# Sums of the second down product's weights made in DRAM by accumulating DMAs from GpSimd's queue

## What is computed

```python
# first block
ffn = silu(h2 @ w_ffn_gate) * (h2 @ w_ffn_up) @ w_ffn_down      # (512, 2816) @ (2816, 1024)
x = x + gate2 * ffn
# second block, whose x is the final norm of the first
u = causal_dwconv(rms_norm(h, ffn_norm) @ w_up, conv_w, conv_b)
gate, up = split(u, 2)
h = h + (silu(gate) * up) @ w_down                              # (512, 2816) @ (2816, 1024)
```

## Time and profile before

| | |
|---|---|
| time, median of 3 runs | 1522.67 us (1521.63 to 1524.0) |
| span of the profiled execution | 1520.9 us |
| PE busy | 1499.2 us, 99% |
| DVE busy | 1026.8 us, 68% |
| ACT busy | 661.2 us, 43% |
| POOL busy | 46.2 us, 3% |
| mean granted clock | 0.998 |
| moved by DMA | 229.29 MB, all of the program's own on one queue |

### The profile page before, as it was taken

The page is one execution under the profiler, slowest core; times in us unless marked ns, Lnnn a source line. Parts: engine busy times, 40 slices in busy tenths (PEclk is TensorE's granted clock), DMA queues, the critical chain, the costliest instruction groups (busy, mean ns, idle before and its releaser), DMA issues.

```text
span 1520.9 us, 21091 instructions
## 1 busy us (share of the span) xinstructions
PE 1499.2 (99%) x8527; PEld 1224.3 (80%) x8527; DVE 1026.8 (68%) x1773; ACT 661.2 (43%) x1090; POOL 46.2 (3%) x82
## 2 busy tenths in 40 slices
PE   7999999999999999999999999999999999999999
PEld 5777888778888898888888777777788988888887
DVE  6679886766588666444459876787567456556885
ACT  4453334653222342222246553766525434434653
POOL 0000000000000000000000021200011000000000
PEclk9999999999999999999999999999999999999999
DMA  9423122149778457665535515100113232232473
GB/s 385 146 83 97 56 70 84 57 181 343 271 267 307 153 187 285 233 222 200 201 127 184 180 60 222 56 30 29 57 56 129 93 107 85 86 111 97 135 229 128
DMA packets 77210, 229.29 MB, mean 151 GB/s; under 512 B 6453, under 2 KB 6581, under 8 KB 75961
## 3 DMA queue, kind: packets, MB, share of 16 engines
q1 hardware_dynamic: 77112, 227.94, 42.9%
HBM read 202.75 MB, written 25.17 MB: 150 GB/s over the span
## 4 chain that ended last, share of the span: by engine, by line
PE 91%; DVE 5%; ACT 3%; issue 1%; POOL 0%; DMA 0%; SPq 0%; DVEq 0%; ACTq 0%
PE bank L696 86%; PE bank L708 4%; DVE AR L1922 1%; DVE wl L1900 1%; ACT wh L1376 0%; DVE G L1929 0%; DVE AR L2232 0%; DVE X L1922 0%; DVE Hl L1922 0%; DVE X L1929 0%; ACT AR L1387 0%; DVE ST L1922 0%; DMA CST<-in_cst 0%; ACT AR L1399 0%; ACT AR L1774 0%
## 5 line engine op out<-in xcount | busy, mean ns | idle before, releaser
L1376 ACT ACTIVATE wh<-raw 128x1024 fp32r<-128x1024 f32 (+1 forms) x223 | 230.6, 1035 | 363.2 <-PE bank L696 317.7
L1900 DVE TENSOR_TENSOR wl<-raw,wh 128x1024 fp32r<-128x1024 f32 (+1 forms) x223 | 263.7, 1192 | 91.7 <-ACT wh L1376 91.6
L696 PE MATMUL bank<-wh,Hh 128*128 128x512 f32 (+1 forms) x726 | 293.1, 404 | 3.8 <-DVE wl L1900 2.5
L696 PE MATMUL bank<-wh,Hl 128*128 128x512 f32 (+1 forms) x726 | 281.1, 387 | 0.0
L696 PE MATMUL bank<-wl,Hh 128*128 128x512 f32 (+1 forms) x726 | 280.3, 386 | 0.0
L696 PE MATMUL bank<-Hh,wh 128*128 128x512 f32 (+2 forms) x712 | 268.5, 377 | 0.2
L696 PE MATMUL bank<-Hl,wh 128*128 128x512 f32 (+2 forms) x712 | 266.9, 375 | 0.0
L696 PE MATMUL bank<-Hh,wl 128*128 128x512 f32 (+2 forms) x712 | 266.9, 375 | 0.0
L696 PEld LDWEIGHTS bank<-wh,Hh 128*128 128x128 f32 x726 | 136.5, 188 | 38.6 <-issue 9.7
L696 PEld LDWEIGHTS bank<-wh,Hl 128*128 128x128 f32 x726 | 136.3, 188 | 28.5
L696 PEld LDWEIGHTS bank<-wl,Hh 128*128 128x128 f32 x726 | 136.8, 188 | 23.4
(11 more groups left out here) (271 smaller groups left out, 2022.2 us busy)
## 6 DMA issues: line engine op xcount, KB each, us to landing
raw<-in_wst SPq DMA_DIRECT2D x224, 512.0 KB, 4.2
CST<-in_down SPq DMA_DIRECT2D x22, 1024.0 KB, 5.9
sums_dram<-CST SPq DMA_DIRECT2D x22, 1024.0 KB, 4.8
raw<-sums_dram SPq DMA_DIRECT2D x40, 512.0 KB, 3.9
raw<-in_down SPq DMA_DIRECT2D x30, 512.0 KB, 3.6
AR<-in_wst SPq DMA_DIRECT2D x8, 1024.0 KB, 11.3
X<-in_x SPq DMA_DIRECT2D x8, 512.0 KB, 6.0
AR<-in_wst SPq DMA_DIRECT2D x5, 512.0 KB, 5.3
```

The source lines that it names most:

```text
L696: return e.matmul(o, l, r, start=start, stop=stop, skip_group_check=True)
L1376: e.activation(HI[slot[i]][:, 0:width(i)], raw[:, i % NR, 0:width(i)], ACT.Copy).then_inc(*w_hi.mark(i))
L1900: e.tensor_tensor(LO[slot[i]][:, 0:n], raw[:, i % NR, 0:n], HI[slot[i]][:, 0:n].bitcast(f32), SUB).then_inc(*w_lo.mark(i))
```

## The change

The sums of `dn` are made as before at the same ticks, but with other signs: all sums are now plain additions, so that b22+b12, b12+b11, b11+b12+b22 and the sum of all four are stored. The signs are made up for on the left factor (one instruction of `left_sum` takes another form, for product "6") and where products are added. The same holds for `2dn`.

The 11 pairs of `2dn` are no longer loaded, summed and stored by SP and DVE. In their place GpSimd issues 11 DMAs from DRAM to DRAM, after the four roots of n2. Each moves one block of all 11 pairs: 1408 rows of 512 floats, 2816 KB. Four are copies (`kept[z]` is the place in `sums_dram` of the sum z). After a wait for all four, four DMAs with `accum_op=ADD` add a second block to what is there; after a wait for these, two more add a third, and after a wait for these one adds the fourth. GpSimd does nothing else in between. SP waits for all of them (`s_kept`, 112) before its first load of a sum of `2dn`.

```diff
@@ summing
-    todo = [(key, p) for key in SEVEN for p in range(11)]
-    early = [k for k, t in enumerate(ticks) if t[0] in EARLY]
-    late = [k for k, t in enumerate(ticks) if t[0] == "up" and t[1][0] > 0]
-    for among, every, after in ((early, 12, 6), (late, 10 / 3, 2)):
...
+    among = [k for k, t in enumerate(ticks) if t[0] in EARLY]
+    for p in range(11):
+        load[among[12 * p]].append(("dn", p))
+        add[among[12 * p + 6]].append(("dn", p))
+        store[among[12 * p + 6]].append(("dn", p))
@@ stored
-            return s_sums, 16 * (11 * SEVEN.index(key) + p + 1)
+            return (s_sums, 16 * (p + 1)) if key == "dn" else (s_kept, 112)
@@ right_sums
-                tt(b22, b22, b12, SUB)
+                tt(b22, b22, b12, ADD)
                 own()
-                tt(b12, b12, b11, SUB)
+                tt(b12, b12, b11, ADD)
                 tt(b11, b11, b22, ADD)
                 own()
-                tt(b21, b21, b11, SUB, ("right sums", key, p))
+                tt(b21, b21, b11, ADD, ("right sums", key, p))
@@ left_sum
-                a, b = {"6": (group("4", u), group("7", u)), "5": (group("1", u), group("6", u)), "3": (group("2", u), group("6", u))}[z]
-                tt(group(z, u), a, b, ADD if z == "5" else SUB, (key, "left sum", z, u))
+                if z == "6":
+                    stt(group(z, u), group("7", u), -1.0, group("4", u), MUL, SUB, (key, "left sum", z, u))
+                else:
+                    tt(group(z, u), group({"5": "1", "3": "2"}[z], u), group("6", u), ADD, (key, "left sum", z, u))
@@ pool_program
+            quarters = down_in[1].rearrange("(a q p) (h c) -> q h a p c", q=2, p=P, h=2)
+            kept = {z: sums_dram[1, i] for i, z in enumerate(SUMMED)}
+            def copies():
+                for z, q in (("7", (1, 1)), ("5", (0, 1)), ("6", (0, 1)), ("4", (0, 1))):
+                    e.dma_start(kept[z], quarters[q]).then_inc(s_halves, 16)
+            def second_terms():
+                on.wait_ge(s_halves, 64)
+                for z, q in (("7", (0, 1)), ("5", (0, 0)), ("6", (0, 0)), ("4", (0, 0))):
+                    e.dma_start(kept[z], quarters[q], accum_op=ADD).then_inc(s_kept, 16)
+            def third_terms():
+                on.wait_ge(s_kept, 64)
+                for z in "64":
+                    e.dma_start(kept[z], quarters[1, 1], accum_op=ADD).then_inc(s_kept, 16)
+            def fourth_term():
+                on.wait_ge(s_kept, 96)
+                e.dma_start(kept["4"], quarters[1, 0], accum_op=ADD).then_inc(s_kept, 16)
...
                 root(ST[:, 16 + t:17 + t], act.of(("n2", "mean", t)), ("n2", "root", t))
+            copies()
+            second_terms()
+            third_terms()
+            fourth_term()
```

More of the change, by code:

```diff
@@ L418, in program @@
         s_cst, s_cst2, s_prm, s_bc, s_out = (sem(n) for n in ("s_cst", "s_cst2", "s_prm", "s_bc", "s_out"))
-        s_pair, s_sums = sem("s_pair"), sem("s_sums")
+        s_pair, s_sums, s_halves, s_kept = (sem(n) for n in ("s_pair", "s_sums", "s_halves", "s_kept"))
         s_in = [sem(f"s_in{t}") for t in range(T)]
@@ L605, in stored @@
         def stored(key, p):
-            return s_sums, 16 * (11 * SEVEN.index(key) + p + 1)
+            return (s_sums, 16 * (p + 1)) if key == "dn" else (s_kept, 112)
         def pair_in(key, p):
-            return s_pair, 16 * (11 * SEVEN.index(key) + p + 1)
+            return s_pair, 16 * (p + 1)
         def group(z, u):
@@ L2443, in added @@
                 on.wait_ge(*dense.of(("dn", z, r)))
-                tt(to, a, bank[BANKS[z][r]][:, :], ADD, ("dn", event, r))
+                b = bank[BANKS[z][r]][:, :]
+                if z in "53":
+                    tt(to, b, a, SUB, ("dn", event, r))
+                else:
+                    tt(to, a, b, ADD, ("dn", event, r))
             for s, z, g, rows in w.steps("dn"):
@@ L2457, in vector_program @@
                         on.wait_ge(*act.of(("dn", "u", r)))
-                        tt(SGR[2 + r], SGR[2 + r], SGR[r], ADD)
+                        tt(SGR[2 + r], SGR[2 + r], SGR[r], SUB)
                         gated(SGR[2 + r], 1, 2 + r)
@@ L2794, in add_product @@
                 xs = X[:, 2 * h + r, 512 * n:512 * n + 512]
-                tt(xs, xs, bank[BANKS[z][r]][:, :], ADD, ("2dn", event, r))
+                tt(xs, xs, bank[BANKS[z][r]][:, :], SUB if z in "76" and n == 1 else ADD, ("2dn", event, r))
             ADDED_AT = {14: ("7", "c22 7", 1, 1), 16: ("1", "c11 1", 0, 0), 20: ("2", "c11", 0, 0), 26: ("5", "c22 5", 1, 1),
```

## The result

The changed kernel takes 1526.51 us (median of 12 runs, 1525.13 to 1527.88) against 1522.31 us of the kernel before (12 runs, 1521.63 to 1524.0). The ratio is 1.0026, 95% interval 1.0017 to 1.0034: **slower by 4 us**, more than the runs scatter. The prediction had 1522.6 us and no change as likeliest, at 0.61.

The account below looks back on a forecast made before the run. PE was taken to bound the kernel, with DVE off the path; removal, other forms, contention and new waits each summed as 0, so 1520.9 us of span stayed, forecast as 1522.6 us measured, range 1519 to 1550.

Parts of the forecast that it names:

- What bounds, and what the removal is worth: Whole kernel and `up`: PE bounds; removing 30.4 us of DVE sums and SP's 22 transfers is worth 0 us.
- Rival 4: Behind `dn`: the 2.58 us stall and slow matmuls shrink by 3 to 4 us, giving 1519; chance 0.06.
- The bytes' price: Eleven new DMAs: between 91 and 149 us of all 16 engines; 149 taken, an accumulating one at two copies.
- how long these 145 us last: New DMAs from 536.4: 149 us over a free share of 0.68 is 219 us, last sum at about 755.
- rival 1: New DMAs on 11 engines take 216 us, 64 remaining in `dn`, where loads starve: +24 us, 1547; chance 0.20.
- an exception: The skill page's direct copies issued by GpSimd that took 16 engines despite the divisor rule; forecast stayed at 16.
- The cover in `up`: Loads in `up` have at least 19.4 us from issue to need; 15 us landings cost PE nothing: 0 us.
- Rival 3: Early `up`, 545 to 600: landings rise beyond 15 us and loads starve, +24 us; chance 0.05.
- The cover in `dn`: Loads in `dn` under 11 crowded engines: cover 10.9 us less about 2.6, and an 11 us lead before PE loses.
- GpSimd's roots: Roots after `dn`, first at 872.31: POOL is free near 740, 130 us early, so cost 0.
- rival 2: Accumulating costs three copies' time on 11 engines, or slow descriptors delay roots after `dn`: about +50 us, 1573; chance 0.08.
- The form of DVE's instruction: Three-operand instructions in `left_sum`, at the start of `dn` and `2dn`: bounds 0 and +0.4 us, taken as 0.

Follow-up runs that it names:

- signs: Kernel before with only the new signs and forms on DVE, no DMA from GpSimd: 1522.39 us, ratio 0.9999 to before.
- wide: Changed kernel with each DMA written as 128 rows of 11 blocks instead of 11 blocks of 128 rows: 1523.06 us, ratio 1.0002 to before.
- longer: Changed kernel with one more copy and one more accumulating DMA, equally narrow, behind the eleventh: 1544.25 us, ratio 1.0143 to before.
- later: Changed kernel with its DMAs moved: copies behind nq's roots, second terms behind `lroot`, the rest behind n4's roots: 1576.82 us, ratio 1.0355 to before.
- wide_later: Changed kernel with DMAs as 128 rows of 11 blocks, copies behind nq's roots, all accumulating DMAs behind n4's: 1522.25 us, ratio 1.0000 to before.
- wide_longer: Changed kernel with DMAs as 128 rows of 11 blocks, plus a copy and three accumulating DMAs more: 1534.46 us, ratio 1.0074 to before.

## Why the prediction was wrong

The forecast was "no change", and the kernel is slower by 4.2 us. Step by step:

- **What bounds, and what the removal is worth**: right. 27.7 us less of DVE and 22 transfers less of SP give 0: `signs` (with that work) and `wide` (without) take the same time. Rival 4 did not come.
- **The bytes' price**: right. The bound that I took said 149 us of 16 engines. The new queue's share is 9.5% of 1524.8 us, 145 us. From the rows below I estimate some 252 us of one engine for an accumulating DMA, in either form (share x 16 x length of the stretch, for 2.88 MB), and 134 us for a wide copy: 1.9 copies, where I had taken 2.
- **The step that failed: how long these 145 us last.** I divided by the free share of all 16 engines, 219 us, and put the last landing at 755. (The 10 us of hand-overs that I named beside it never went into that sum.) In the form that spreads widely the sum was good: 748.5. In the changed kernel's form it took 275 us, to 810. That was **rival 1**, given 0.20, with the decision point "about 150 us on the busiest engine by 760". Its time of 1547 was for transfers over the rest of `dn`; they were over at 810, so the price was 4.2 us and not 24. `longer`, whose transfers do run to 866, paid 22. The row that would have decided, a transfer with 11 as outermost count, did not exist in the trace. It does in the runs. GpSimd's queue where a single transfer is under way and next to no loads run (packets, MB, share of 16 engines): a narrow accumulating one (`later`, 1315 to 1323 us), a wide one (`wide_later`, 1302 to 1310), a narrow copy (`longer`, 814 to 817) and a wide one (`wide_longer`, 751 to 757).

```profile
q0 software_dynamic: 559, 1.14, 77.7%
q0 software_dynamic: 802, 1.64, 112.4%
q0 software_dynamic: 328, 0.77, 67.1%
q0 software_dynamic: 519, 2.13, 103.2%
```

  The accumulating ones moved 1.14 and 1.64 MB in 8 us, 143 and 205 GB/s. Rates and shares both stand as 0.69 to 1, and 11/16 is 0.69. (A share can pass 100%: the times of packets overlap.) The copies' shares stand as 0.65 to 1. The loads show it directly. A load's landing is 16 events in the trace. For the load issued at 792.7 in the changed kernel, five of them come by 797.3 and eleven from 803.2 to 805.0; for its fellow in the kernel before, issued at 793.4, all 16 come from 796.6 to 797.8. So eleven engines were crowded and five were not.
- **Where the 64 us between 211 and 275 arose**: 7 with the copies, 31 with the second terms, 13 with the third and 13 with the eleventh DMA. Two narrow transfers at once do fill all 16 engines (in the changed kernel the queue's share is 112.6% from 732 to 736 us, beside no loads), so rival 1's sum, with all eleven transfers on the same 11 engines, is not what happened. The time goes where a transfer is alone, and at the end of a group, when one engine still works and GpSimd is held.
- **The chance that I gave it.** The Trainium skill ("DMA: Bandwidth & Descriptors", Why a DMA increments its semaphore by 16 and not by 1) had the rule, and I set the forecast against it on the strength of an exception; I should have given rival 1 the larger chance. The rows above agree with the rule's 11 for the copies too, so the exception did not apply here.
- **The cover in `up`**: right. Landings at the start rose to 13.5 us (`wide`: 14.1) and PE never waited. Rival 3 did not come.
- **The cover in `dn`**: the mechanism was right, "4 x 2.72 = 10.9 us less about 2.6" against a median landing of 9.3 us, and a lead of 11 us that it eats. Two things were left out. From the last late landing to PE's matmul it took 5.2 us (808.86 to 814.09) and not 2.6, because other instructions of `dn` stood in the queues of ACT and DVE. And once PE had idled for 2.5 us, it ran at the lower clock for 3.4 us, which cost 1.7 us more.
- **GpSimd's roots**: right for the changed kernel. The first root came 4.0 us later than before, with ACT as its releaser, as late as PE was (4.0 us). But "rival 2", a root that comes late since GpSimd is held, is a real mechanism: `later` paid some 54 us for it. I had put it on slow descriptors or slow sums; it was a hold of GpSimd's queue at an accumulating DMA, which no wait in the program shows.
- **The form of DVE's instruction** at 0: right (`signs`).

## What to carry to other kernels

Moving work off an engine that nobody waits for won nothing here and could only cost; ask how long its replacement stays on the shared resource and which later stage it meets there. When a background transfer is priced, divide by the engines that its shape reaches, write it so that the outermost count has 16 as a divisor, and let it end before the stage whose loads have the least slack, for the cost is no steady tax but begins when a lead has been eaten up. Never queue anything that is waited for behind several accumulating DMAs on GpSimd.

## What the runs showed of the hardware

- A transfer of 2816 KB from DRAM added to DRAM, alone on the DMA engines: 143 GB/s as 11 blocks of 128 rows, 205 GB/s as 128 rows of 11 blocks. From issue to landing the two took 33.2 and 19.2 us, but these are not alike: beside the first 4.0 MB of loads were moved, beside the second 1.3 MB.
- Beside such a transfer of 11 blocks, the 16 landing events of a load fell apart into five early and eleven some 6 us later.
- GpSimd was held at an accumulating DMA until those before it had landed, for 67 to 86 us (narrow) and 18 to 22 us (wide), without a semaphore in the program; at the fourth in the narrow form, at the sixth in the wide one. Plain copies, up to five in a row, were never held. The cause is open.
- An idle time of 2.5 us on PE was followed by 3.4 us at the lower clock, in the changed kernel at 814 us as behind `dn` in both kernels.
- In `up` of `wide`, PE stayed fully busy beside a DMA share of 0.97; its loads of 512 KB landed in 14.1 us at most. In `dn`, with half the time between chunks, landings of 5.6 to 12.3 us made it wait.
